# Two transformer blocks on one core: order of block 2's opening steps, and GpSimd for the scaling of attention probabilities

## What is computed

```python
def hybrid_layer(h, ...):
    h = h + 0.5 * swiglu(rmsnorm(h, ffn1_norm), ...)
    u = rmsnorm(h, mix_norm); z = u @ w_in
    m_qk, m_v, m_o, m_i, m_f, a_q, a_k, a_v, g_m, g_a = jnp.split(z, offs, axis=-1)
    m_qk = jax.nn.silu(causal_dwconv(m_qk, m_conv_w, m_conv_b))
    ...
    hm = sigmoid(m_o) * head_rmsnorm(mlstm_chunkwise(mq, mk, mv, ig, lf), m_out_norm)
    aq = head_rmsnorm(a_q, a_q_norm); ak = head_rmsnorm(a_k, a_k_norm)   # 16 and 4 heads, 64 wide
    ha = swa_gqa_sinks(aq, ak, a_v, a_sinks)      # window of 128, sink logits
    merged = sigmoid(g_m) * (hm @ w_branch_m) + sigmoid(g_a) * (ha @ w_branch_a)
    h = h + merged @ w_out
    ...

# in swa_gqa_sinks, 128 queries against two blocks of 128 keys
    mx = jnp.maximum(jnp.max(scores, -1), sink)
    pr = jnp.exp(scores - mx)
    den = jnp.sum(pr, -1) + jnp.exp(sink - mx)
    attn = pr / den                               # "even" in the kernel
    out = einsum(attn, v)
```

## Time and profile before

| | us |
|---|---|
| median of three runs (2297.05 to 2297.55) | 2297.5 |
| the profiled execution's own time | 2293.15 |
| its span | 2291.4 |
| TensorE busy, of the span | 2278.3 (99%) |
| VectorE busy | 1533.0 (67%) |
| ScalarE busy | 1232.8 (54%) |
| GpSimd busy | 134.6 (6%) |
| granted TensorE clock | full in all of the 40 slices |

### The profile page before, as it was taken

How to read it: one execution, slowest core, us unless ns; L and a number is a source line. 1 busy time by engine, 2 the same in 40 slices (tenths; PEclk the granted TensorE clock), 3 DMA queues, 4 the chain that set the end, 5 groups by cost and what they waited for, 6 DMA issues and landing times.

```text
span 2291.4 us, 30120 instructions
## 1 busy us (share of the span) xinstructions
PE 2278.3 (99%) x11144; PEld 1902.6 (83%) x11144; DVE 1533.0 (67%) x2411; ACT 1232.8 (54%) x1890; POOL 134.6 (6%) x141
## 2 busy tenths in 40 slices
PE   9999999999999999999999999999999999999999
PEld 8887888888888888888888888888888888888887
DVE  6667786566687866676487666664765687657654
ACT  6556444445555444355467754554544477645443
POOL 3140000013220000000000000000000000000000
PEclk9999999999999999999999999999999999999999
DMA  8556568756485587487564444875677564456772
GB/s 337 197 181 257 192 230 293 225 184 211 148 293 192 184 278 240 164 274 248 188 232 154 165 153 160 270 244 195 220 239 239 180 221 157 148 175 204 233 238 87
DMA packets 179857, 483.08 MB, mean 211 GB/s; under 512 B 20480, under 2 KB 65152, under 8 KB 178688
## 3 DMA queue, kind: packets, MB, share of 16 engines
q1 hardware_dynamic: 179712, 481.16, 62.8%
HBM read 452.24 MB, written 28.84 MB: 210 GB/s over the span
## 4 chain that ended last, share of the span: by engine, by line
PE 94%; DVE 3%; DMA 1%; ACT 1%; issue 1%; SPq 0%; DVEq 0%; ACTq 0%
PE bank L2113 28%; PE bank L2118 27%; PE bank L2117 27%; PE bank L2160 2%; PE bank L2100 2%; PE bank L2101 2%; PE bank L2102 2%; DMA raw<-in_weights 1%; DVE wl L1602 1%; PE bank L2249 1%; PE bank L2211 0%; PE bank L2182 0%; PE bank L2234 0%; ACT wh L1372 0%; SPq L1190 0%
## 5 line engine op out<-in xcount | busy, mean ns | idle before, releaser
L1372 ACT ACTIVATE wh<-raw 128x1024 fp32r<-128x1024 f32 (+1 forms) x778 | 813.6, 1051 | 774.7 <-PE bank L2118 684.1
L1602 DVE TENSOR_TENSOR wl<-raw,wh 128x1024 fp32r<-128x1024 f32 (+1 forms) x778 | 932.7, 1229 | 271.0 <-ACT wh L1372 267.8
L2113 PE MATMUL bank<-wh,xh 128*128 128x512 f32 (+1 forms) x2102 | 825.8, 393 | 5.3 <-issue 4.0
L2118 PE MATMUL bank<-wh,xl 128*128 128x512 f32 (+1 forms) x2102 | 815.9, 388 | 0.0
L2117 PE MATMUL bank<-wl,xh 128*128 128x512 f32 (+1 forms) x2102 | 814.9, 388 | 0.0
L2113 PEld LDWEIGHTS bank<-wh,xh 128*128 128x128 f32 x2102 | 394.7, 188 | 86.9 <-issue 7.8
L2118 PEld LDWEIGHTS bank<-wh,xl 128*128 128x128 f32 x2102 | 394.5, 188 | 81.1
L2117 PEld LDWEIGHTS bank<-wl,xh 128*128 128x128 f32 x2102 | 394.9, 188 | 77.1
L2113 PE MATMUL bank<-wh,act_h 128*128 128x512 f32 x528 | 205.9, 390 | 0.0
L2118 PE MATMUL bank<-wh,act_l 128*128 128x512 f32 x512 | 199.3, 389 | 0.0
L2117 PE MATMUL bank<-wl,act_h 128*128 128x512 f32 x512 | 199.3, 389 | 0.0
(11 more groups left out here) (347 smaller groups left out, 2068.5 us busy)
## 6 DMA issues: line engine op xcount, KB each, us to landing
raw<-in_weights SPq DMA_DIRECT2D x760, 512.0 KB, 4.3
turn<-ffn_s SPq DMA_DIRECT2D x264, 64.0 KB, 2.8
ffn_a<-turn SPq DMA_DIRECT2D x66, 256.0 KB, 4.6
raw<-in_weights SPq DMA_DIRECT2D x16, 384.0 KB, 3.4
ln<-in_ln SPq DMA_DIRECT2D x4, 1024.0 KB, 7.5
moved<-merged SPq DMA_DIRECT2D x32, 128.0 KB, 6.6
merged<-moved SPq DMA_DIRECT2D x8, 512.0 KB, 5.3
bias<-in_bias SPq DMA_DIRECT2D x2, 1024.0 KB, 8.6
```

The costliest lines, as they stand in the source:

```text
L1372: act.activation(wh[:, u % NH, 0:used(u)], raw[:, u % NR, 0:used(u)], ACT.Copy).then_inc(hi_done, 1)
L1602: dve.tensor_tensor(wl[:, u % NR, 0:used(u)], raw[:, u % NR, 0:used(u)], wh[:, u % NH, 0:used(u)].bitcast(F32), ALU.subtract).then_inc(lo_ ...
L2113: pe.matmul(out, h, w_h, start=st.first and i == 0, stop=False)
L2118: last = pe.matmul(out, lo, w_h, start=False, stop=ends)
```

## The change

- The tables are written in another form: for every side step the number of units of the stretch that come before it (`PLACES_1`, `PLACES_2`), and `weave` sorts the side steps by that. So the steps of one kind need no longer stand in the order in which they were planned. In both layers of block 1 this sets the steps of the differential attention (`da_s`, `da_mix`, `probs_T`, `da_pv`) one unit later; all else in block 1 keeps its place.
- In both layers of block 2 the root chain is a step of its own, `a_root`, behind the first convolved chunk's `conv`.
- The moves of the last queries (`block`, `out`, `back`, `copy` of `aq1`) go into the weave: transposed behind unit 8 of it, stored behind 9, loaded behind 11, copied behind 15. `m_spread` goes from unit 4 to 9.
- `gain_ffn2` is loaded behind the two gate chunks instead of ahead of them.
- GpSimd scales the probabilities of the 64-wide heads of block 2: two products a pair of heads in place of ScalarE's four instructions, and both heads are released at the end.

```diff
-UNITS_AMONG_1 = "0101110101110001100001010111012101001101011210111000111212311002101010201102243"
-UNITS_AMONG_2 = "100110300011211002110001101011110011110401001111100100111101101000101020040102"
+PLACES_1 = (0, 1, 1, 2, 3, 4, 4, 5, 5, 6, 7, 8, 8, 8, 8, 9, 10, 10, 10, 10, 10, 11, 11, 12, 12, 13, 14, 15, 15, 16,
...
+PLACES_2 = (1, 1, 1, 2, 2, 3, 8, 9, 11, 15, 6, 9, 6, 7, 8, 10, 11, 12, 12, 12, 14, 15, 16, 16, 16, 16, 17, 18, 18,
...
+    def weave(self, before, dense, side, places):
+
+        assert len(places) == len(side), (len(places), len(side))
         self.steps = before
...
+        left = sorted(zip(places, side), key=lambda pair: pair[0])
+        done = 0
+        for st in dense:
+            if st.kind == "unit":
+                while left and left[0][0] <= done:
+                    self.steps.append(left.pop(0)[1])
...
+                done += 1
+            self.steps.append(st)
+        self.steps += [sd for _, sd in left]
...
             if name == "aq0":
                 p.add("a_knorm")
                 p.moved("block", "ak")
-            p.moved("block", name, kept=q[name])
+                p.moved("block", "aq0", kept=q["aq0"])
...
     p.moved("back", "aq0")
-    p.moved("out", "aq1")
...
-    p.add("load", name="gain_ffn2", n=p.cc["mgated"])
...
     g_a = [gate2("ha", 6664, j, None) for j in range(2)]
+    p.add("load", name="gain_ffn2", n=p.cc["mgated"])
...
-    for name in ("ak", "aq0", "aq1"):
-        if name == "aq1":
-            p.moved("back", name)
-        c_a = p.moved("copy", name)
+    p.add("a_root")
+    for name in ("ak", "aq0"):
+        p.moved("copy", name)
+    for what in ("block", "out", "back", "copy"):
+        c_a = p.moved(what, "aq1", kept=q["aq1"])
...
+                    elif st.kind == "even" and st.of == "aa":
+                        n = st.h
+                        pool.wait_ge(shares, st.m)
+                        for r in (1, 0):
+                            part = b["Pn"][:, n % 4:n % 4 + 2, 0:256] if r else b["Pn"][:, n % 4:n % 4 + 2, 256:384]
+                            last = pool.tensor_tensor(part, part, of2(rc, n)[:, 2 * r:2 * r + 2].unsqueeze(2)
+                                                      .broadcast_to([P, 2, 256 if r else P]), ALU.mult)
+                        last.then_inc(evened, 2)
...
-                    elif k == "even" and st.of == "aa":
-                        act.wait_ge(shares, st.m)
-                        for i in range(2):
-                            for r in (1, 0):
-                                part = b["Pn"][:, (st.h + i) % 4, 0:256] if r else b["Pn"][:, (st.h + i) % 4, 256:384]
-                                at = 2 * (st.h % 8) + 2 * r + i
-                                last = act.activation(part, part, ACT.Copy, scale=rc[:, at:at + 1])
-                            last.then_inc(evened, 1)
...
-                        if r == R - 1:
-                            dve.wait_ge(summed, R * (st.l + 1))
-                            rsqrt(R * AH, ssq[:, 8:8 + R * AH], 1.0, ADH * EPS, rq2)
+                    elif k == "a_root":
+                        dve.wait_ge(summed, R * (st.l + 1))
+                        rsqrt(R * AH, ssq[:, 8:8 + R * AH], 1.0, ADH * EPS, rq2)
```

More of the change, by code:

```diff
@@ L38 @@
 WARM = (3, 3)
-UNITS_AMONG_1 = "0101110101110001100001010111012101001101011210111000111212311002101010201102243"
-UNITS_AMONG_2 = "100110300011211002110001101011110011110401001111100100111101101000101020040102"
+PLACES_1 = (0, 1, 1, 2, 3, 4, 4, 5, 5, 6, 7, 8, 8, 8, 8, 9, 10, 10, 10, 10, 10, 11, 11, 12, 12, 13, 14, 15, 15, 16,
+            18, 19, 19, 20, 20, 20, 21, 22, 22, 23, 23, 24, 25, 27, 28, 28, 29, 30, 31, 31, 31, 31, 32, 33, 34, 36,
+            37, 40, 43, 44, 45, 45, 45, 47, 48, 48, 49, 49, 50, 50, 52, 52, 53, 53, 53, 55, 57, 61)
+PLACES_2 = (1, 1, 1, 2, 2, 3, 8, 9, 11, 15, 6, 9, 6, 7, 8, 10, 11, 12, 12, 12, 14, 15, 16, 16, 16, 16, 17, 18, 18,
+            19, 19, 20, 21, 22, 23, 23, 23, 24, 25, 26, 27, 27, 31, 31, 32, 32, 32, 33, 34, 35, 36, 37, 37, 37, 38,
+            38, 38, 39, 40, 41, 42, 42, 43, 44, 44, 45, 45, 45, 45, 46, 46, 47, 47, 49, 49, 49, 53, 53, 54, 54)
 TAILS = {"branch_c": (4, 1, 2, 3), "w_out_1": (8, 6, 5, 5), "ffn_1": (10, 5, 4, 6), "branch_m": (8, 5, 3, 5),
@@ L169, in begin @@
         return kept
-    def weave(self, before, dense, side, table):
-        dense = list(dense)
-        def take(n):
-            while dense and (n > 0 or dense[0].kind != "unit"):
-                st = dense.pop(0)
-                if st.kind == "unit":
-                    assert not any(sd.t is not None and sd.t == st.after_t for sd in left), st.u
-                    assert not any(sd.kind == "o_split" and sd.o + 1 == st.after_o for sd in left), st.u
-                    n -= 1
-                self.steps.append(st)
-        assert len(table) == len(side) + 1, (len(table), len(side))
-        self.steps = before
-        left = list(side)
-        take(int(table[0]))
-        for sd, n in zip(side, table[1:]):
-            left.pop(0)
-            self.steps.append(sd)
-            take(int(n))
-        take(len(dense))
+    def weave(self, before, dense, side, places):
+        assert len(places) == len(side), (len(places), len(side))
+        self.steps = before
+        left = sorted(zip(places, side), key=lambda pair: pair[0])
[4 more added lines that the diff above has]
+                    self.steps.append(left.pop(0)[1])
+                assert not any(sd.t is not None and sd.t == st.after_t for _, sd in left), st.u
+                assert not any(sd.kind == "o_split" and sd.o + 1 == st.after_o for _, sd in left), st.u
+                done += 1
+            self.steps.append(st)
+        self.steps += [sd for _, sd in left]
     def flip(self):
@@ L474, in plan_block1 @@
         merge(1, j, "w_branch_b", "ob", 4, j, ob_o + 1)
-    p.weave(before, dense_a + p.begin(), side, UNITS_AMONG_1)
+    p.weave(before, dense_a + p.begin(), side, PLACES_1)
     kept = p.begin()
@@ L760, in plan_block2 @@
     g_m = [gate2("hm", 5640, j, c_a[j]) for j in range(2)]
-    p.weave(before, dense_a + p.begin(), side, UNITS_AMONG_2)
+    p.weave(before, dense_a + p.begin(), side, PLACES_2)
     kept = p.begin()
```

## The result

| | before | after |
|---|---|---|
| median of 7 executions each, us | 2296.98 | 2303.25 |
| lowest and highest, us | 2292.83, 2297.55 | 2301.10, 2304.89 |
| profiled execution, its own time, us | 2293.15 | 2304.89 |
| its span, us | 2291.4 | 2303.2 |

The ratio is 1.003, with a 95% interval from 1.0019 to 1.0042: slower by 6.3 us on the medians, 2303.25 where 2306.4 was forecast. The two profiled executions are 11.7 us apart, because before's was one of its shorter ones and this one is the longest of seven.

What follows compares the result with a forecast made beforehand. TensorE bounds the kernel, busy 2278.3 of 2291.4 us. Terms summed as 2 x (-1.9 + 2.2 + 4.1) + 0.1 = 8.9 us, added to 2297.5: 2306.4 us; 8-in-10 range 2296 to 2318.

Steps and rivals of the forecast that it cites:

- term 3: Block 2, GpSimd's scaling: TensorE waits before transposes, mostly heads 2 and 3; +4.1 us a layer, from +1 to +8.
- term 2: Block 2, scores of heads 4 and 5: TensorE waits for late copies of transposed heads; +2.2 us a layer, +1.0 to +2.6.
- term 1: Block 2, first convolved chunk: TensorE's 2.0 us wait near 1190 goes; -1.9 us a layer, between 0 and -2.0.
- term 4: Block 1: kT wait goes (-1.1), first mix waits 0.6 in both layers; +0.1 us, from -1.5 to +1.5.
- Hidden: Last queries' stores, loads and copy, second gain's later load, and root's first reader: covered, no wait on TensorE.
- the port decides everywhere: Rival: each GpSimd product loses a turn to VectorE, 2 us a step, 6 us a layer more; 2318 us, chance 0.20.
- The covers hold: Rival, decided at heads 2 and 3: VectorE's taps not late, GpSimd ends before TensorE arrives; 2293.8 us, chance 0.14.

Runs made afterwards that it cites:

- after_pick_late: The changed kernel with `m_spread` four units later; 2301.60 us against 2294.79 for the kernel before, ratio 1.0025.
- block1_only: The kernel before with the changed kernel's `PLACES_1` (block 1 places) and nothing else; 2296.80 us against 2294.96, ratio 1.0007.
- root_only: The kernel before with only the root chain moved behind the first convolved chunk in both layers of block 2; 2295.83 us against 2294.96, ratio 0.9999.
- late_start: The kernel before with block 2's root chain, first attention scores, `m_spread` and some later steps placed later, ScalarE scaling; 2291.82 us against 2294.92, ratio 0.9987.
- moves_only: The changed kernel with the root chain back ahead of the first `conv` and ScalarE scaling; 2297.24 us against 2294.96 for the kernel before, ratio 1.0006.
- root_gpsimd: The kernel before with the root chain behind the first convolved chunk and GpSimd's scaling; 2300.37 us against 2294.30, ratio 1.0023.
- root_even2: root_only with the even step of heads 2 and 3 one unit earlier; 2301.25 us against 2294.30 for the kernel before, ratio 1.0024.
- best1: root_even2 with GpSimd scaling and, in block 1, only the first scores one unit later; 2296.15 us against 2294.30 for the kernel before, ratio 1.0009.
- late_start_b1: late_start with block 1's first differential attention scores one unit later; 2291.06 us against 2294.92 for the kernel before, ratio 0.9981.
- late_start_b1_pool: late_start_b1 with GpSimd's scaling; 2293.58 us against 2294.92 for the kernel before, ratio 0.9995.
- after_act: The changed kernel with ScalarE's scaling put back; 2299.66 us against 2294.30 for the kernel before, ratio 1.0022.

## Where the prediction was right and where not

The time, 2303.25, lies in the range, and slower was the likeliest case. By the second layer of block 2 less its 1.5 us of lowered clock, taken twice, and block 1's 1.2, the changed kernel is 2 x 3.7 + 1.2 = 8.6 us longer than before's undisturbed profile; the sum said 8.9. The main mechanism is shown: TensorE comes earlier, its helpers do not, and it waits at the places that were named. That the sum is so near is in part luck: term 3 was 1.1 us a layer too high, term 2 0.35 and term 1 0.1 a layer too low, and term 4 1.1 too low, and these cancel. Term by term:

- **Term 1**, -1.9 a layer: -1.74 and -1.84. Right.
- **Term 2**, +2.2: the scores wait 2.05 us, the first product with the values 0.35; with the transitions 2.12 and 0.42 in both layers, 2.55. Place, order and cause as drawn, and `pick`'s 0.85 is shown as 0.75 by after_pick_late. The size is near the top of its range: the first copy lands 0.4 us later than forecast (1218.89, less the 1.32 us by which this profile's block 2 begins later, against 1217.2), and TensorE comes only 0.15 later.
- **Term 3**, +4.1: heads 2 and 3 2.45 where the clock had not fallen before (2.7 forecast), heads 6 and 7 0.55 (0.8), heads 14 and 15 and the other five pairs at most 0.1 (0.6): 3.0. The price of a step, 1.9, was neither of the two that occur, 1.6 and 2.5 to 2.6; at heads 2 and 3 it was 0.3 too high and the reciprocal came 0.3 later than drawn, so that GpSimd's end, 1228.92 - 1.32 = 1227.6, met the forecast of 1227.5 by two errors. Of the five pairs a layer that lost a turn only heads 6 and 7 show it on TensorE; at the others it fitted into the cover.
- **Term 4**, +0.1: +1.2 in block1_only, 1.5 in the changed kernel's profile. The step that failed is "it waits 0.6, in both layers": the mix costs 0.77 (0.60 and the transition), and the last head's product with the values, which moved by the same unit, 0.39 more in each layer, for which no row had been read.
- **Hidden** work: the last queries' stores, loads and copy, the later gain load and the root's first reader show nowhere as a wait. Right.
- **Not in the prediction: the clock.** Two stretches at 1.2 GHz slow TensorE by 3.0 us in this profile. They did not make the forecast wrong, because a lowered clock ahead of a wait is taken out of that wait (0.68 instead of 2.27), so that 1.5 is left, and because other executions of before have such stretches too (block1_only's profile, whose block 2 is before's, has one), with no wait behind them to hide in.
- **The base.** The medians are 6.3 us apart, not 8.6. Before's seven executions have a median of 2296.98; in the four later groups, of 17 to 35 executions each, it was 2294.3 to 2295.0, from which 2303.25 is 8.3 to 9.0 us away. Those groups ran on four different chips, so whether this is chance or the chip is open. The forecast added its sum to 2297.5; added to 2294.96, the median of the largest group, the same sum gives 2303.9. So the 3 us between 2306.4 and 2303.25 need no error in the sum.

Of the rivals, "the port decides everywhere" asked for 6 us more a layer and the runs have none of it: GpSimd's lost turns happen (10 of the 16 pairs, 0.9 us each), VectorE's small steps lose one (0.92 us), but only where there is no cover does it reach TensorE. The rule of the Trainium skill ("SBUF — State Buffer", section on the two separate sides), that the shared port pair is held for a whole instruction, agrees with the 0.92 us multiply, which ends when `pick` does, and with the 1.63 us split. "The covers hold" fell at heads 2 and 3 in every run in which the root chain moved and the attention did not.

The theory stated with the runs, that TensorE was given time that its helpers did not have, held in root_only and late_start by the places and order of the waits. Sizes worked out from it often did not hold: root_only missed the 1.2 us before the fourth convolved chunk, moves_only has half of what was expected, root_gpsimd 1.2 us a layer more, and in root_even2 and best1 the next queue behind the freed one was not followed; their signs were wrong. Left open is which of late_start's shifts are needed; they were only run together.

## What to carry to other kernels

A wait of the bound engine that goes is a loan: the helpers behind it get their work no earlier than before, and must be walked pair by pair until one of them has idle time. Here moving 2.9 us of VectorE work out of the way removed a wait of 1.75 us and bought nothing; starting the first attention steps one or two units later, so that ScalarE did other work in its idle time ahead of them instead of behind them, kept 1.3 to 1.5 us of it. And work handed to an engine that releases only at its end was free in these runs only where a cover at least as long as its duration stood ahead of the reader.

## What the chip showed that was not expected

A wait of TensorE can cost more than its length. In block1_only, whose block 2 is that of before, the same 2.0 us wait of the first layer was followed by this (windows; the granted clock is the last column but two):

```profile
1188.00:1192.00 4.00, 3.71 (x31) 3.51 (x30) 3.69 (x11) 4.00 (x7) 0.00 (x0) 1.00 1.02 387
1192.00:1196.00 4.00, 2.31 (x6) 1.88 (x7) 3.93 (x7) 3.82 (x6) 0.00 (x0) 0.72 0.74 284
1196.00:1200.00 4.00, 4.00 (x17) 3.25 (x16) 3.86 (x8) 1.06 (x1) 0.00 (x0) 0.86 0.18 42
```

and C is 1.60 us longer than in before's profile, for nothing but the clock. In the profiles here it fell to 1.2 GHz behind waits of 1.7 us (the kT wait of late_start) to 2.7, each time at a loss of 1.5 to 1.6 us to TensorE, and not behind every one of them (before's profile has two of 2.0 us and no fall; after_pick_late's two of 2.3); behind shorter waits no profile has it. Why it falls in some executions and not in others is open. It shows in the times as well. The 35 executions of before in the first group of runs, by their mean granted clock: 13 at 1.000 with a mean of 2293.8 us, 17 at 0.999 with 2295.6, 5 at 0.998 with 2299.3. Kernels with no wait over 1.5 us in their profile had 1.000 nearly always: moves_only in 12 of 12 executions, best1, late_start_b1 and late_start_b1_pool in 11 of 11, after_act in 9 of 11. The changed kernel had it in none of 7.

So before's mean carries some 1.6 us of lowered clock (the mean of the 35 is 2295.4, against 2293.8), and a kernel that cuts its 2 us waits to 1.5 wins this on top. It fits that moves_only and root_only look better by their times than by their stretches: with executions at 1.000 alone, moves_only is 3.3 us and root_only 2.0 us over before, where their stretches give 3.0 and 2.0. And late_start_b1 is 2.7 us faster so, where its stretches of block 2 give 2.8, and not 3.9. The other part that varies is the kT wait, 1.1 to 2.7 us in the profiles of kernels that have it.
